# Stick-breaking heads as a sum over value differences, with the stick values projected last

## The reference

```python
def stick_breaking_attention(q, k, v):
    ...
    def block(i):
        z = jnp.einsum('bhqd,bhkd->bhqk', qb, k).astype(jnp.float32) * scale
        q_idx = start + jnp.arange(BLOCK_Q)
        mask = k_idx[None, :] < q_idx[:, None]
        log_beta = jax.nn.log_sigmoid(z)
        log_1m_beta = jnp.where(mask, jax.nn.log_sigmoid(-z), 0.0)
        suffix = lax.cumsum(log_1m_beta, axis=3, reverse=True) - log_1m_beta
        a = jnp.where(mask, jnp.exp(log_beta + suffix), 0.0)
        return jnp.einsum('bhqk,bhkd->bhqd', a.astype(v.dtype), v)
```

## Time and profile before

| what | value |
|---|---|
| median of three runs | 2158.98 us |
| the profiled execution: time, span of its records | 2163.58 us, 2161.7 us |
| TensorE busy, share of the span | 1979.8 us, 92% |
| VectorE, ScalarE, GpSimd busy | 829.9, 501.9, 1116.5 us |
| mean granted clock of TensorE | 0.959 |
| chain that ended last: PE, DVE, ACT, POOL | 82%, 9%, 3%, 2% |

### The profile page before, as it was taken

The page is one execution under the profiler, slowest core; times in us unless marked ns, Lnnn a source line. Parts: engine busy times, 40 slices in busy tenths (PEclk is TensorE's granted clock), DMA queues, the critical chain, the costliest instruction groups (busy, mean ns, idle before and its releaser), DMA issues.

```text
span 2161.7 us, 29403 instructions
## 1 busy us (share of the span) xinstructions
PE 1979.8 (92%) x10416; PEld 1604.6 (74%) x10416; DVE 829.9 (38%) x1453; ACT 501.9 (23%) x1253; POOL 1116.5 (52%) x731
## 2 busy tenths in 40 slices
PE   5777899789999998987799999999999899999999
PEld 4666566578888887874478888887787578888887
DVE  4763667554535105545723222102453623212100
ACT  2111466322222102225511010101132511101100
POOL 4434001157666663622746666666553446666663
PEclk9887899699999998999899999999999999999999
DMA  4212000123333231312013333332321113333332
GB/s 135 59 57 88 0 0 4 37 88 98 97 97 115 89 102 56 89 34 69 11 50 98 97 97 96 94 95 76 83 85 59 41 40 92 97 96 95 97 97 88
DMA packets 125373, 161.99 MB, mean 75 GB/s; under 512 B 11670, under 2 KB 87398, under 8 KB 125286
## 3 DMA queue, kind: packets, MB, share of 16 engines
q1 hardware_dynamic: 121440, 159.97, 24.2%
q10 hardware_dynamic: 3846, 0.82, 0.2%
HBM read 158.66 MB, written 2.10 MB: 74 GB/s over the span
## 4 chain that ended last, share of the span: by engine, by line
PE 82%; DVE 9%; ACT 3%; issue 2%; POOL 2%; DMA 1%; ACTq 0%; SPq 0%; DVEq 0%; POOLq 0%
PE ps L718 22%; PE ps L720 22%; PE ps L719 22%; PE ps L1156 3%; PE ps L1085 2%; PE ps L1177 2%; PE ps L733 2%; PE ps L851 1%; PE ps L1168 1%; DVE tok L1827 1%; PE ps L1274 1%; PE ps L1126 1%; PE ps L1061 1%; DVE xt_lo L1837 1%; ACT dump L1395 1%
## 5 line engine op out<-in xcount | busy, mean ns | idle before, releaser
L447 POOL TENSOR_TENSOR w_lo<-raw,w_hi 128x1024 fp32r<-128x1024 f32 (+1 forms) x256 | 614.7, 2401 | 21.4
L445 POOL TENSOR_SCALAR w_hi<-raw 128x1024 fp32r<-128x1024 f32 (+1 forms) x256 | 275.4, 1076 | 574.0 <-PE ps L720 497.3
L718 PE MATMUL ps<-xt_hi,w_hi 128*128 128x512 f32 (+1 forms) x1160 | 432.9, 373 | 7.2 <-DVE xt_lo L1837 6.5
L720 PE MATMUL ps<-xt_hi,w_lo 128*128 128x512 f32 (+1 forms) x1160 | 432.2, 373 | 0.0
L719 PE MATMUL ps<-xt_lo,w_hi 128*128 128x512 f32 (+1 forms) x1160 | 432.2, 373 | 0.0
L718 PE MATMUL ps<-w_hi,xt_hi 128*128 128x512 f32 (+3 forms) x672 | 264.1, 393 | 28.7 <-ACT tok L1666 20.0
L720 PE MATMUL ps<-w_hi,xt_lo 128*128 128x512 f32 (+3 forms) x672 | 259.1, 386 | 0.0
L719 PE MATMUL ps<-w_lo,xt_hi 128*128 128x512 f32 (+3 forms) x672 | 258.9, 385 | 0.0
L718 PEld LDWEIGHTS ps<-xt_hi,w_hi 128*128 128x128 f32 x1160 | 219.2, 189 | 47.0 <-DVE xt_lo L1837 7.6
L720 PEld LDWEIGHTS ps<-xt_hi,w_lo 128*128 128x128 f32 x1160 | 219.0, 189 | 38.7
L719 PEld LDWEIGHTS ps<-xt_lo,w_hi 128*128 128x128 f32 x1160 | 219.2, 189 | 38.3
(11 more groups left out here) (317 smaller groups left out, 2480.3 us busy)
## 6 DMA issues: line engine op xcount, KB each, us to landing
raw<-in_w_up SPq DMA_DIRECT2D x88, 256.0 KB
raw<-in_l_w_gate SPq DMA_DIRECT2D x88, 256.0 KB
raw<-in_l_w_up SPq DMA_DIRECT2D x88, 256.0 KB
raw<-in_l_w_down SPq DMA_DIRECT2D x40, 512.0 KB
raw<-in_l_w_in SPq DMA_DIRECT2D x36, 512.0 KB
raw<-in_w_down SPq DMA_DIRECT2D x20, 512.0 KB
raw<-in_l_w_o SPq DMA_DIRECT2D x16, 512.0 KB
raw<-in_w_in SPq DMA_DIRECT2D x12, 512.0 KB
```

What stands on the lines that cost most here:

```text
L445: e.tensor_scalar(w_hi[:, s, 0:width], r, 1.0, 0.0, ALU.mult, ALU.add).then_inc(split, 1)
L447: e.tensor_tensor(w_lo[:, s, 0:width], r, w_hi[:, s, 0:width].bitcast(F32), ALU.subtract).then_inc(split, 1)
L718: e.matmul(o, s_hi, m_hi, start=start, stop=False)
L720: return e.matmul(o, s_lo, m_hi, start=False, stop=stop)
```

## The change

1. **In2's order** becomes CQ, SQ, Q0, SK, Q1, K0, K1, SV. Q1, K0 and K1 are turned after slabs 1, 2 and 3 of SV. VectorE does the norms of K0 and K1 before the copies of turned Q1, K0, K1. K0 and K1 are staged in `tok_k`, two buffers of their own.
2. **Places.** `km_a` gets room of its own, `km_b` lies in `gains`; `inv_t`, `o_sb` of mix and the new `v_back` lie in the halves of `xt_hi`, `xt_lo` where `km_a`, `km_b` were. So SyncE loads gains 6 and 7 only after the last softmax scores (`mix_s` 16), behind the first group of out2's slabs.
3. **Mix's start** waits only for K0's turned keys; K1's are waited for in round 1.
4. **Value differences.** ScalarE issues two transfers from `v2` to `v_back`, 1 MB in all, each row one token back; GpSimd sets row 0 to zero and subtracts `v_back` from `v2` in four instructions of 128x512, ahead of `pool_pairs`. The first `values` of a stick pair waits for them (`v_step`).
5. **No differences of runs.** VectorE's running product writes over its input. `runs`, its memsets and GpSimd's 32 subtractions go. The stick copies of turned tiles become 1 - x (Identity with scale -1 and bias 1 on ScalarE; multiply and add on VectorE).
6. **Who copies.** For stick steps with g%4 = 2 or 3 VectorE takes half y = 0, seven copies more than before.

```diff
     IN2 = [(416, 0, 4, 2), (512, 4, 4, 2), (384, 8, 1, 2), (512, 9, 4, 2), (384, 13, 1, 2), (512, 14, 1, 1),
-           (512, 15, 4, 2), (512, 19, 1, 1)]
-    CQ, SQ, Q0, SK, Q1, K0, SV, K1 = range(8)
+           (512, 15, 1, 1), (512, 16, 4, 2)]
+    CQ, SQ, Q0, SK, Q1, K0, K1, SV = range(8)
...
-        gain_load(e, 6, at("in2_tp", 27))
+        sp_group(e, ph["out2"].g0, two_kt(A["l0_w_o_2"], 0, W))
+        gain_load(e, 6, at("mix_s", 16))
         gain_load(e, 7)
-        with e.Fori(0, 2) as c:
-            sp_group(e, c + ph["out2"].g0, two_kt(A["l0_w_o_2"], c * W, W))
+        sp_group(e, ph["out2"].g0 + 1, two_kt(A["l0_w_o_2"], W, W))
...
-        def sticks(g):
-            for x in range(2):
-                u = 2 * (g - 4 * st.soft) + x + 1
-                e.wait_ge(*at(f"{name}_sc", u))
-                r = run_at(g, x)
-                n = (4 - g % 4) * P
-                e.tensor_tensor(prob_at(g, x), r[:, 1:n + 1], r[:, 0:n], ALU.subtract).then_inc(sem(f"{name}_w"), 1)
...
+        e.wait_ge(*at("in2_copy", 32))
+        e.memset(v_back[0:1, 0, :], 0.0).then_inc(sem("v_first"), 1)
+        e.wait_ge(*at("v_first", 1))
+        e.wait_ge(*at("v_back", 32))
+        for t in range(NT):
+            e.tensor_tensor(v2[:, t, W:D], v2[:, t, W:D], v_back[:, t, :], ALU.subtract).then_inc(sem("v_step"), 1)
         pool_pairs(e, mix, {3 + 4 * s: (ph["out2"].g0, s) for s in range(4)})
...
-        return "d" if y == 0 and g == 4 * st.soft + 3 else "a"
+        return "d" if y == 0 and g % 4 >= 2 else "a"
...
-                e.wait_ge(*at(f"{name}_w", 2 * (g - 4 * st.soft) + 2))
+                e.wait_ge(*at(f"{name}_sc", 2 * (g - 4 * st.soft) + 2))
...
+            if p == st.soft:
+                e.wait_ge(*at("v_step", NT))
...
+            if r == 1:
+                for s, v in later:
+                    e.wait_ge(s, v)
...
-                   {(SQ, 2): (CQ,), (Q0, 0): (SQ,), (SK, 2): (Q0,), (Q1, 0): (SK,), (SV, 1): (Q1,), (SV, 3): (K0,)},
+                   {(SQ, 2): (CQ,), (Q0, 0): (SQ,), (SK, 2): (Q0,), (Q1, 0): (SK,), (SV, 1): (Q1,), (SV, 2): (K0,), (SV, 3): (K1,)},
...
-        pe_pair_attend(e, mix, mix_scores, heads_of(v2), [at("in2_tpa", 12), at("in2_tpd", 15), at("in2_copy", 32)], [])
+        pe_pair_attend(e, mix, mix_scores, heads_of(v2), [at("in2_tpa", 10), at("in2_tpd", 13), at("in2_copy", 32)], [],
+                       [at("in2_tpa", 12), at("in2_tpd", 15)])
...
+                        op = e.activation(turned_probs(st, g, y), turned_bank(g, y), ACT.Identity, scale=-1.0, bias=1.0)
...
         def high(p):
             e.wait_ge(*at(f"{name}_o", p + 1))
+            if p == st.soft:
+                e.wait_ge(*at(f"{name}_lo", st.soft))
...
+        e.wait_ge(*at("in2_copy", 32))
+        e.dma_start(v_back[1:P, :, :], v2[0:P - 1, :, W:D]).then_inc(sem("v_back"), 16)
+        e.dma_start(v_back[0:1, 1:NT, :], v2[P - 1:P, 0:NT - 1, W:D]).then_inc(sem("v_back"), 16)
         act_pair_attend(e, od, mix)
...
-                if h >= 4:
-                    e.wait_ge(*at(f"{name}_w", 2 * (h - 4) + x + 1))
-                e.tensor_tensor_scan(run_at(g, x)[:, 0:n][:, ::-1], prob_at(g, x)[:, ::-1],
-                                     one[:, 0:1].broadcast_to([P, n]), 1.0, ALU.mult, ALU.mult).then_inc(
+                keep = prob_at(g, x)[:, ::-1]
+                e.tensor_tensor_scan(keep, keep, one[:, 0:1].broadcast_to([P, n]), 1.0, ALU.mult, ALU.mult).then_inc(
                     *od.done(*at(f"{name}_sc", 2 * h + x + 1)))
...
+                        op = e.tensor_scalar(turned_probs(st, g, y), turned_bank(g, y), -1.0, 1.0, ALU.mult, ALU.add)
...
-        for step in (CQ, SQ, (Q0,), Q0, SK, (Q1,), (K0,), Q1, K0, (K1,), K1):
+        for step in (CQ, SQ, (Q0,), Q0, SK, (Q1,), (K0,), (K1,), Q1, K0, K1):
```

More of the change, by code:

```diff
@@ L181, in build @@
     sb("under_first", [P, 4, SEQ], F32, lay)
-    km_a = sb("km_a", [MQK, 4, SEQ], F32, lay)
+    inv_t2 = sb("inv_t2", [P, 2, SEQ], F32, lay)
+    o_sb2 = sb("o_sb2", [P, 2, SEQ], F32, lay)
     sb("under_second", [P, 4, SEQ], F32, lay)
-    km_b = sb("km_b", [MQK, 4, SEQ], F32, lay)
+    v_back = sb("v_back", [P, NT, W], F32, lay)
     lay.close()
@@ L224, in build @@
     u = ExitStack()
[L225 to L231, removed]
+    qm = sb("qm", [MQK, 8, SEQ], F32, u)
     qs = sb("qs", [P, 4, SEQ], F32, u)
@@ L234, in build @@
     v2 = sb("v2", [P, NT, D], F32, u)
+    km_a = sb("km_a", [MQK, 4, SEQ], F32, u)
     o_ = ExitStack()
@@ L239, in build @@
     cq_lo = sb("cq_lo", [P, 2, SEQ], F32R, o_)
+    tok_k = [sb(f"tok_k{i}", [P, NT, 4 * MQK], F32, o_) for i in range(2)]
     o_.close()
-    mix_rooms = dict(p_turn=sb("p_turn2", [P, 2, 2, 13, P], F32, u), inv_t=sb("inv_t2", [P, 2, SEQ], F32, u),
-                     o_sb=sb("o_sb2", [P, 2, SEQ], F32, u), inv_w=sb("inv_w2", [P, 8, HD], F32, u),
-                     inv=sb("inv2", [P, 8], F32, u))
+    mix_rooms = dict(p_turn=sb("p_turn2", [P, 2, 2, 13, P], F32, u), inv_t=inv_t2, o_sb=o_sb2,
+                     inv_w=sb("inv_w2", [P, 8, HD], F32, u), inv=sb("inv2", [P, 8], F32, u))
     u.close()
@@ L283, in build @@
         "p (k s c) -> p k s c", k=2, s=CMPS)
-    tok_b = gains[:, :, :].rearrange("p a n -> p (a n)")[:, 0:NT * 4 * MQK].rearrange("p (t n) -> p t n", t=NT)
+    km_b = gains[0:MQK, :, :].rearrange("p a (k n) -> p (a k) n", n=SEQ)
     xn = tok[:, 0:2 * D].rearrange("p (s n) -> p s n", s=2)
@@ L526, in build @@
     mix = Pairs("mix", 4, 8, mix_rooms)
[L528 to L533, removed]
     def pool_pairs(e, st, slabs):
@@ L664, in staged @@
     def staged(name, c):
-        return tok_b if name == "in2" and c == K0 else tok3
+        return tok_k[c - K0] if name == "in2" and c in (K0, K1) else tok3
     def alternate(items, scale=None):
@@ L690, in build @@
         mla_heads(km_a, 0, 1),
+        mla_heads(km_b, 0, 1),
         [],
-        mla_heads(km_b, 0, 1),
     ]
@@ L1035, in output_free, with pe_pair_attend @@
         return at(f"{st.name}_x", p + 1) if p < st.soft else at(f"{st.name}_slo", p + 1 - st.soft)
-    def pe_pair_attend(e, st, score, value, start, banks):
+    def pe_pair_attend(e, st, score, value, start, banks, later=()):
         name = st.name
@@ L1605, in turned @@
                     e.wait_ge(*at(f"{name}_t", g + 1))
-                    e.activation(turned_probs(st, g, y), turned_bank(g, y), ACT.Copy).then_inc(
-                        *od.done(*is_turned(st, g, y)))
+                    if st.is_soft(g):
+                        op = e.activation(turned_probs(st, g, y), turned_bank(g, y), ACT.Copy)
+                    else:
+                        op = e.activation(turned_probs(st, g, y), turned_bank(g, y), ACT.Identity, scale=-1.0, bias=1.0)
+                    op.then_inc(*od.done(*is_turned(st, g, y)))
         def inverses(p):
@@ L1745, in _ @@
         for c in range(8):
-            act_copies(e, od, "in2", c, ends[c], copy2(c), plan, c not in (K0, SV))
+            act_copies(e, od, "in2", c, ends[c], copy2(c), plan, c not in (K0, K1, SV))
             if c == CQ or c in HEAD_CHUNKS:
                 act_rstd(e, od, "in2", 1 if c == CQ else HEAD_CHUNKS[c] + 2, 8 if c == CQ else 16)
-            for x in {Q1: (), K0: (Q1, K0), SV: ()}.get(c, (c,)):
+            for x in {Q1: (), K0: (), K1: (Q1, K0), SV: (K1,)}.get(c, (c,)):
                 act_turned(e, od, "in2", plan, x)
+        e.wait_ge(*at("in2_copy", 32))
+        e.dma_start(v_back[1:P, :, :], v2[0:P - 1, :, W:D]).then_inc(sem("v_back"), 16)
+        e.dma_start(v_back[0:1, 1:NT, :], v2[P - 1:P, 0:NT - 1, W:D]).then_inc(sem("v_back"), 16)
         act_pair_attend(e, od, mix)
@@ L2069, in turned @@
                     e.wait_ge(*at(f"{name}_t", g + 1))
-                    e.tensor_copy(turned_probs(st, g, y), turned_bank(g, y)).then_inc(*od.done(*is_turned(st, g, y)))
+                    if st.is_soft(g):
+                        op = e.tensor_copy(turned_probs(st, g, y), turned_bank(g, y))
+                    else:
+                        op = e.tensor_scalar(turned_probs(st, g, y), turned_bank(g, y), -1.0, 1.0, ALU.mult, ALU.add)
+                    op.then_inc(*od.done(*is_turned(st, g, y)))
         def turned_inverse(p):
@@ L2092, in dve_pair_attend @@
         for r in st.rounds:
-            if r == 4 * st.soft and r < st.steps:
-                e.wait_ge(*at(f"{name}_s", r + 1))
-                for g in range(r, r + 4):
-                    n = (4 - g % 4) * P
-                    e.memset(runs[:, :, RUN_AT[g % 4] + n:RUN_AT[g % 4] + n + 1], 1.0).then_inc(*od.own())
             if r < st.steps:
```

7 lines of the change are left out of this document (2 added, 5 removed).

## The result

The changed kernel takes 2195.73 us (median of four, 2193.70 to 2197.07), beside 2160.02 us for the kernel before in the same session. The ratio is 1.0165, between 1.0147 and 1.0183: **35.7 us slower**, where 2151 was predicted. The profiled execution took 2195.32 us with a span of 2193.6, against 2161.7.

What follows compares the result with a forecast made beforehand. TensorE was taken to bound the kernel, with gaps to win between in2 and mix and in the stick half. Terms -6.2 and -1.5 make -7.7, from 2158.98 to 2151 us; own case 2147 to 2154, with rivals 2143 to 2156.

Steps and rivals of the forecast that it cites:

- Part 2: Start of mix and value differences: transfer lands in 5 to 7.4 us, costing nothing, with 2.9 us to spare.
- The slower rival: Softmax half: `v_back` lands late and TensorE stands in round 9; slower from 18 us, 2164 at 23 us; chance 0.05.
- part 3: Stick half of mix: loop and end terms with ScalarE's bias cost sum to -1.5 us.
- The prediction's sign of being wrong: Start of mix: the prediction is wrong if GpSimd's `widened` comes over 20 us after mix starts.
- ScalarE's two issues hidden: Start of mix: two transfer issues, SyncE's took 0.36 us, hidden by the first exponential's wait of over 3 us.
- Softmax rounds keep their instructions: 0: Softmax half of mix: the rounds keep their instructions, so their time changes by 0.
- Part 1: In2's new order: K1's turn comes behind matmuls at the full clock, so mix starts 6.2 us earlier.
- The loop of VectorE's copy behind its products: Stick half: TensorE's turn 27 and `values` wait for VectorE's copy behind later products; 12.1 us, all lead given back.
- the case that the prediction named as one that would make it wrong: Stick half: TensorE's clock doesn't fall before the late `values`; staying up in both gains 1.7 us each.
- the +0.5 us: Stick half: ScalarE's bias operand costs 0.08 us per turned copy, some six in the path, +0.5 us.
- two products of 256 keys in place: Stick half: VectorE's product in place costs what it did, 0, at most +0.5 us each.
- the end, -2.4: End of stick half: last turns and `values` take 10.7 us instead of 13.1 with GpSimd's differences between, -2.4.

Runs made afterwards that it cites:

- kernel 2: The changed kernel with ScalarE's two issues exchanged, the one-row transfer ahead of the one of 127 partitions; 2195.06 us (one run).
- kernel 1: The changed kernel with the transfer of 127 partitions issued as one of 112 and one of 15; 2156.59 us, ratio 0.998.
- kernel 4: The changed kernel with twelve filler matmuls of 512 columns in round 3, right behind the long wait; 2185.19 us (one run).
- kernel 6: kernel 1 with in2's order and the start of mix as before the change; 2163.82 us, ratio 1.0011.
- kernel 5: kernel 1 with the sharing of stick copies undone, ScalarE making all but one; 2145.29 us, ratio 0.9934.
- kernel 10: kernel 5 with in2's order and the start of mix as before the change; 2154.54 us, ratio 0.9963.
- kernel 3: kernel 2 with GpSimd's wait for the transfer and its four subtractions moved to the first stick round; 2159.76 us, ratio 0.9992.

## Why the prediction was wrong, by its steps

**Part 2 is the step that failed: "The transfer of 1 MB is not in this trace", high value 7.4 us, low 5.** It took 43. The figure came from three loads, 1.5 MB in all, whose tiles all have 128 partitions, and it was carried over by bytes. The row moved back by one makes 127, and the rate is then 26 GB/s against 257 to 309 with the split. The slower rival said that lateness costs from 10.3 us on, and priced 23 us at 2164; it was dismissed with "Nothing in the rows moves 1 MB that slowly". No row showed a transfer of this shape, so the rows excluded nothing: the top of the bound was not a bound. By the rival's own sum 43 us would give 2184; kernel 2 took 2195, as the clock and part 3 came on top. The prediction's sign of being wrong, `widened` over 20 us after mix starts, is met: it comes at 1036.73, 51.6 us after. In kernel 1 it comes 14.8 us after, where 17 was predicted.

**The same part held ScalarE's two issues hidden, at 0.36 us each.** The first took 0.87, the second 33.99. Kernel 2 shows that the order of the two decides whether ScalarE is held (0.81 us with the long transfer issued last), kernel 1 that it isn't the number of issues. The place of the loss was therefore round 2 of mix, through ScalarE, and not round 9, through GpSimd; kernel 2 shows that the rival's place would have cost as much.

**"Softmax rounds keep their instructions: 0"** was right for the instructions and wrong for their clock behind the wait: some 10 us (kernel 4).

**Part 1, -6.2 us, was right: -6.5**, and -7.2 in kernel 6's medians. On the clock of the kernel before, 2.5 us later than the rows of after, SV's tile 3 starts at 963.0 (961.9 predicted), the norms of K1 end at 971.4 (970.2), mix starts at 987.6 (988.0).

**Part 3, -1.5 us: -2.6 in the changed kernel, +1.8 in kernel 1**, from the same instructions. Times from the first stick scores:

| | before | predicted lead | kernel 1 | after |
|---|---|---|---|---|
| turn 20 | 27.2 | -4.8 | 22.1 (-5.0) | 23.1 (-4.1) |
| `values` behind turn 23 end | 37.7 | -3.2 | 33.8 (-3.9) | 33.3 (-4.4) |
| `values` behind turn 27 end | 46.2 | +0.4 | 46.7 (+0.5) | 43.6 (-2.6) |
| from there to out2 | 13.1 | -2.4 | 14.5 (+1.4) | 13.0 (-0.1) |

The loop of VectorE's copy behind its products was predicted at 12.1 us from end to end of `values` at the low clock. In kernel 1 it was 12.9 from end to end and 12.15 from start to start; the mechanism was right. In the changed kernel TensorE waits the same 2.62 and 2.13 us, but the clock stayed up (the case that the prediction named as one that would make it wrong), and a pair takes 10.4:

```profile
1094.89 0.28 PE L1045 MATMUL ps<-ident,tok 64*128 64x64 f32 x2 [2.62 <-DVE p_turn L2069]
1095.24 2.37 PE L1071 MATMUL ps<-p_turn,v 128*64 128x512 f32 x16
...
1105.34 0.28 PE L1045 MATMUL ps<-ident,tok 64*128 64x64 f32 x2 [2.13 <-DVE p_turn L2069]
1105.61 2.37 PE L1071 MATMUL ps<-p_turn,v 128*64 128x512 f32 x16
```

Two smaller terms: a turned copy on ScalarE with its bias takes 395 ns for 256 elements (389 before) and 509 for 384 (509), so the +0.5 us isn't there (the rows compared two different functions); and two products of 256 keys in place take the 1.27 us that they took before, as predicted. One reading was loose: the 3.97 us of the earlier trace rows were called free of most of GpSimd's subtractions, which in fact run beside them from 1073.15 on, 2.7 of the 3.97 us. No term of the sum uses it.

The term of this part that was wrong is the end, -2.4, taken for GpSimd's differences: it measured -0.1, and +1.4 in kernel 1. They were not what held TensorE there. Before and after, from the timelines, the waits are equal, with only the releaser's name changed:

```profile
1079.37 0.28 PE L1061 MATMUL ps<-ident,tok 64*128 64x64 f32 x2 [1.27 <-POOL scratch L560]
1081.01 0.46 PE L1061 MATMUL ps<-ident,tok 64*128 64x64 f32 x8 [1.05 <-POOL tok L560]
```

```profile
1110.29 0.28 PE L1045 MATMUL ps<-ident,tok 64*128 64x64 f32 x2 [1.27 <-ACT p_turn L1599]
1111.93 0.47 PE L1045 MATMUL ps<-ident,tok 64*128 64x64 f32 x8 [1.05 <-ACT p_turn L1599]
```

**What the parts are worth**, by medians: the order 7 to 9 us (kernel 1 against 6, kernel 5 against 10), the value differences 7 (kernel 10), the sharing a loss of 9 to 11 (kernel 5 against 1, 10 against 6), the shape of one transfer a loss of 39. The stretches of the profiles say it more closely: the order -6.5, the differences -7.7, the sharing +9.5 both with the new order (61.1 against 51.6) and with the old (61.1 against 51.5). They add up to -4.7 where kernel 1's ratio gives -4.3. With the split transfer the change came out at 2156.6, above the 2151 predicted and just above the range's 2156. So part 3 had a fault of its own, 3.3 us in kernel 1, most of it the end term. Its sum joined a gain of 7.7 and a loss of 9.5, which only kernels 5 and 10 tell apart. Without the sharing it is 2145.3.

## What to carry to other kernels

A transfer whose shape the trace doesn't show can't be priced by its bytes: look at the partition counts of both sides first, and if tokens are shifted by one, cut the odd rows off (112 and 15 instead of 127). When an engine of the path issues transfers, ask what stands behind the issue, and don't put a second one behind a slow one. A copy moved to another engine is worth what its place in that engine's order makes it: ahead of the long running products it cost 0.8 us of the profiled stick half, behind them 9.5.

## What the hardware showed that I had not expected

- A 6 KB transfer issued behind an unfinished 1 MB one on the same queue held ScalarE's instruction queue for 33.99 us; in the other order both issues took 0.8 us. It was released at 1019.8, some 9 us before the data were in. Which resource it waited for stays open.
- The one-engine transfer took 43 us alone and 53 beside SyncE's slabs (kernel 3).
- After 30 us idle TensorE stayed at 0.50 for some 28 us while busy almost without a gap. Twelve matmuls more in that stretch shortened the softmax half by 5.8 us, their own time included.
- The same waits of 2.62 and 2.13 us left the clock up in one kernel and down in another (`values` 2.37 against 3.83 and 4.53 us). The two kernels differ by the long stall, but that alone isn't it: kernel 2, behind a stall of 33.8 us, has 3.46 and 3.68 us behind waits of 2.02 and 2.13. The cause stays open.
- Fillers that gained 5 us in one profile gained nothing in the median.
